# An FFN unit reads its first kept half before the rounding of its last weight block, every other one into a second buffer

## What is computed

```python
def swiglu(h, w_up, w_down):
    gate, up = jnp.split(h @ w_up, 2, axis=-1)
    return (jax.nn.silu(gate) * up) @ w_down
```

## Time and profile before

| | us |
|---|---|
| median of three runs | 941.75 |
| lowest, highest | 941.49, 942.89 |
| the profiled execution, its own time | 946.19 |
| its span, first to last instruction | 944.4 |
| PE busy | 921.6 (98%) |
| DVE busy | 669.7 (71%) |
| ACT busy | 446.7 (47%) |
| POOL busy | 107.8 (11%) |

### The profile page before, as it was taken

The page is one execution under the profiler, slowest core; times in us unless marked ns, Lnnn a source line. Parts: engine busy times, 40 slices in busy tenths (PEclk is TensorE's granted clock), DMA queues, the critical chain, the costliest instruction groups (busy, mean ns, idle before and its releaser), DMA issues.

```text
span 944.4 us, 22445 instructions
## 1 busy us (share of the span) xinstructions
PE 921.6 (98%) x9425; PEld 894.1 (95%) x9425; DVE 669.7 (71%) x1254; ACT 446.7 (47%) x824; POOL 107.8 (11%) x135
## 2 busy tenths in 40 slices
PE   5999999999999999999999999999999999999997
PEld 5899888999999999999999999999999999999997
DVE  3678878875567767477766888999435899994454
ACT  6588345423334554663222257565322666653223
POOL 0101011211120110100100001222001222220000
PEclk9999999999999999999999999999999999999998
DMA  9825233434343432315743232332333343323312
GB/s 348 267 67 156 59 88 84 143 104 136 103 129 102 125 87 69 101 47 145 238 124 111 85 96 68 87 93 73 86 97 105 98 119 97 91 78 94 91 51 95
DMA packets 146031, 104.82 MB, mean 111 GB/s; under 512 B 5153, under 2 KB 138855, under 8 KB 144779
## 3 DMA queue, kind: packets, MB, share of 16 engines
q1 hardware_dynamic: 138955, 79.16, 28.7%
q0 software_dynamic: 6352, 22.00, 7.5%
q10 hardware_dynamic: 624, 2.23, 0.6%
HBM read 100.06 MB, written 3.31 MB: 109 GB/s over the span
## 4 chain that ended last, share of the span: by engine, by line
PE 90%; DVE 4%; ACT 3%; issue 2%; DMA 0%; ACTq 0%; DVEq 0%
PE G L2216 58%; PE G L2311 19%; PE R L2224 12%; PE R L2227 1%; DVE cy L1887 1%; DVE cy L1884 1%; DMA xtok<-in_x_prompt 0%; DVE cy L1888 0%; DVE cy L1883 0%; ACT w_hi L1258 0%; DVE w_sum L1752 0%; DVE sum_lo L1761 0%; ACT L1274 0%; DVE relT L1934 0%; ACT inp L1274 0%
## 5 line engine op out<-in xcount | busy, mean ns | idle before, releaser
L2216 PE MATMUL G<-h_hi,w_hi 128*128 128x272 f32 (+1 forms) x880 | 264.4, 300 | 0.2 <-DVE ff_shift L2162 0.2
L2216 PE MATMUL G<-h_lo,w_hi 128*128 128x272 f32 (+1 forms) x880 | 254.5, 289 | 0.4 <-issue 0.4
L2216 PE MATMUL G<-h_hi,w_lo 128*128 128x272 f32 (+1 forms) x880 | 254.2, 289 | 0.0
L1645 DVE TENSOR_TENSOR w_lo<-raw,w_hi 128x1024 fp32r<-128x1024 f32 (+3 forms) x111 | 118.6, 1069 | 82.1 <-ACT w_hi L1258 81.4
L2216 PEld LDWEIGHTS G<-h_hi,w_hi 128*128 128x128 f32 x880 | 166.5, 189 | 3.2 <-DVE ff_shift L2162 0.4
L2216 PEld LDWEIGHTS G<-h_lo,w_hi 128*128 128x128 f32 x880 | 166.7, 189 | 0.6 <-issue 0.6
L2216 PEld LDWEIGHTS G<-h_hi,w_lo 128*128 128x128 f32 x880 | 166.4, 189 | 0.0
L1258 ACT ACTIVATE w_hi<-raw 128x1024 fp32r<-128x1024 f32 (+3 forms) x111 | 101.5, 914 | 114.1 <-PE G L2216 113.9
L2311 PE MATMUL G<-x_hi,sum_hi 128*128 128x272 f32 x288 | 83.8, 291 | 1.6 <-ACT partial L1369 1.5
L2311 PE MATMUL G<-x_hi,sum_lo 128*128 128x272 f32 x288 | 83.4, 290 | 0.0
L2311 PE MATMUL G<-x_lo,sum_hi 128*128 128x272 f32 x288 | 83.0, 288 | 0.0
(11 more groups left out here) (335 smaller groups left out, 2117.2 us busy)
## 6 DMA issues: line engine op xcount, KB each, us to landing
raw<-in_w_in SPq DMA_DIRECT2D x48, 512.0 KB, 4.1
raw<-in_w_up SPq DMA_DIRECT2D x44, 512.0 KB, 4.0
w_ada<-in_w_ada_t POOLq DMA_DIRECT2D x49, 256.0 KB, 3.2
wada<-in_w_ada_s SPq DMA_DIRECT2D x8, 1024.0 KB, 14.3
raw<-in_w_down SPq DMA_DIRECT2D x14, 384.0 KB, 3.4
raw<-in_w_down SPq DMA_DIRECT2D x16, 320.0 KB, 3.2
raw<-in_w_out SPq DMA_DIRECT2D x8, 512.0 KB, 4.0
w_ada_t<-in_w_ada_t POOLq DMA_DIRECT2D x15, 256.0 KB, 3.2
```

The source lines that it names most:

```text
L1645: dve.tensor_tensor(lo, raw[:, i % RAW, 0:job.nk, 0:job.m], hi.bitcast(F32), ALU.subtract).then_inc(w_lo_done, 1)
L2216: ins = pe.matmul(out, w, x, start=(job.first and k == 0 and p == 0), stop=(job.last and k == job.nk - 1 and p == 2))
```

## The change

Reading 0 moves ahead of the rounding of `d` and of `q_ahi` in all units (it stood there in unit 1). Odd units keep it in `acc[:, 0:272]` instead of `partial[:, 0, :]`, so reading 0 of unit u waits for `q_c11` of unit u-2 instead of unit u-1. In unit 0, reading 3 goes ahead of the rounding of sum 2 of unit 1 (and of its sum and of the low part of sum 1, which are on VectorE).

```diff
             for p in range(len(PRODUCTS)):
                 do("q_mul", u, p)
-            if u == 1:
-                do("q_read", u, 0)
+            do("q_read", u, 0)
             if u > us[0]:
                 do("q_a", u - 1, 0)
                 do("q_hi", u, "d")
                 do("q_ahi", u - 1)
                 do("q_lo", u, "d")
                 do("q_alo", u - 1)
-            if u != 1:
-                do("q_read", u, 0)
             if soon:
                 do("q_read", u, 1)
...
             if not soon:
                 do("q_read", u, 2)
+            if u == 0:
+                do("q_read", u, 3)
             if nxt is not None:
                 do("q_add", nxt, 2)
                 do("q_lo", nxt, 1)
                 do("q_hi", nxt, 2)
             do("q_c12", u)
-            if soon:
+            if u == 1:
                 do("q_read", u, 3)
...
+        def kept(u, r):
+
+            return acc[:, 0:HALF] if r == 0 and u % 2 else partial[:, r, :]
...
                     act.wait_ge(q_done, 7 * u + READS[r] + 1)
-                    if u:
-                        act.wait_ge(q_out, 3 * (u - 1) + (3, 2, 1, 2)[r])
-                    else:
+                    before = u - (2 if r == 0 else 1)
+                    if before >= 0:
+                        act.wait_ge(q_out, 3 * before + (3, 2, 1, 2)[r])
+                    elif u == 0:
                         wait_slot(act, groups_before[0] - 1)
-                    act.activation(partial[:, r, :], q_bank(u, "y" if r == 1 else "x"), ACT.Copy).then_inc(q_kept, 1)
+                    act.activation(kept(u, r), q_bank(u, "y" if r == 1 else "x"), ACT.Copy).then_inc(q_kept, 1)
```

More of the change, by code:

```diff
@@ L1766, in _ @@
                     dve.wait_ge(q_kept, 4 * u + 3)
-                    dve.tensor_tensor(q_halves(g_act[:, u % 2, :])[1], q_bank(u, "y"), partial[:, 2, :], ALU.add)\
+                    dve.tensor_tensor(q_halves(g_act[:, u % 2, :])[1], q_bank(u, "y"), kept(u, 2), ALU.add)\
                         .then_inc(q_out, 1)
@@ L1771, in _ @@
                     dve.wait_ge(q_kept, 4 * u + 4)
-                    dve.tensor_tensor(q_halves(val[:, a_no(u) % 2, :])[1], partial[:, 3, :], partial[:, 1, :], ALU.add)\
+                    dve.tensor_tensor(q_halves(val[:, a_no(u) % 2, :])[1], kept(u, 3), kept(u, 1), ALU.add)\
                         .then_inc(q_out, 1)
@@ L1776, in _ @@
                     dve.wait_ge(q_done, 7 * u + 6)
-                    dve.tensor_tensor(q_halves(g_act[:, u % 2, :])[0], q_bank(u, "z"), partial[:, 0, :], ALU.add)\
+                    dve.tensor_tensor(q_halves(g_act[:, u % 2, :])[0], q_bank(u, "z"), kept(u, 0), ALU.add)\
                         .then_inc(q_out, 1)
```

## The result

The changed kernel takes 949.94 us median of 6 runs (948.82 to 950.83) against 942.32 us for the kernel before in the same comparison (941.24 to 946.19, 6 runs): a ratio of 1.0074, 95% interval 1.0062 to 1.0085. That is 7.0 us of 942.3, within 5.8 to 8.0.

What follows compares the result with a forecast made beforehand. PE's matmul stream (98% busy) was taken as the bound, with a chain over other engines just longer in steady units. 5.0 + 0.9 + 0.6 = +6.5 us on 941.75 gave 948.2 us, range 945.3 to 950.0.

Steps and rivals of the forecast that it cites:

- The sum: Whole kernel: 5.0 + 0.9 + 0.6 = +6.5 us, giving 948.2 us on the median of 941.75.
- The second buffer, 0: Reading 0 no longer waits for the previous unit's q_c11, but the silu ahead on ACT covers that wait: 0 us.
- Reading 0 ahead of d, +0.50 in ten units: Units 7 to 16: d_hi 0.68 us later, w_lo and product 6 0.50 later; +5.0 us, bounds 4.3 and 6.8.
- the two ways in which DVE and POOL could meet: At POOL's sum 1, steady units: DVE's activation low part first, w_lo 0.50 us later; or POOL first, 0.43 later.
- Units 2 to 4, +0.9: 0.77 us won ahead of unit 2's product 2, but the d chain is delayed as in steady units: +0.9 us.
- the bounds -0.9 and +1.5: Units 2 to 4: three units at -0.3 us each, or at +0.50 us each.
- Reading 3 of unit 0, +0.6: Unit 0's 0.37 us wait at product 6 goes, none kept; unit 1 loses more: +0.6 us, bounds -0.4 and +0.7.
- the predicted pair of gaps: Unit 1: product 2 still waits until about 618.8; product 3 waits till 620.95 and restarts, +0.66 us.
- The first (faster): Gaps at the readings count, later d costs nothing, unit 1's gap goes: about 2.4 us faster, 939.3 us; chance 0.07.
- The second: Steady units lose nothing, DVE and POOL not excluding each other; only unit 2's gap is won: 941.0 us; chance 0.11.
- The third's gap: Gaps at products 3 and 4 add to product 6's, ten times 0.25 us more: 950.7 us; chance 0.08.
- A sign of being wrong, badly put: Units 7 to 16: wrong if product 6's distance stays 10.7 us or POOL's start is independent of DVE's preceding instruction.

Runs made afterwards that it cites:

- e1: The second buffer alone, every step in its old place, against the kernel before: 942.65 us, ratio 0.9994.
- e9: Kernel before plus second buffer; reading 3 before sum 4's rounding, reading 0 between roundings (units 2-5), unit 1's reading 0 before silu, reading 1 before d: ratio 0.9972.
- e2: Reading 0 ahead of the rounding of d in all units, one buffer, reading 3 of unit 0 unmoved, against the kernel before: 948.71 us, ratio 1.0058.
- e4: The changed kernel with d's rounding ahead of reading 0 again, reading 0 still ahead of the activation's rounding: 943.65 us, ratio 1.0008 to the kernel before.
- e8: The changed kernel with the activation's low part moved behind DVE's sum 4 where a unit has a successor: 943.76 us, ratio 1.0013 to the kernel before.
- e3: Only unit 0's reading 3 moved ahead of the rounding, against the kernel before: 943.27 us, ratio 0.9996.
- e10: The changed kernel with reading 1 too ahead of d's rounding in units 2 to 5 and 7 to 17: 970.98 us, ratio 1.0298 to the kernel before.
- e5: The kernel before with reading 3 ahead of the rounding of sum 4: 941.77 us, ratio 0.9993.

## Why the prediction was right

- **The sum.** +6.5 us was predicted from rows of the kernel before; 6.43 us stands in the stages and 7.0 us (5.8 to 8.0) in the comparison. 949.94 lies 1.7 above the predicted 948.2, and 0.6 of that is the median of before, 942.32 here for 941.75. The other 1.1 us does not stand in the stages; the executions of one kernel spread by 2 to 5 us.
- **The second buffer, 0.** Shown by e1: -0.03 us. That the silu covers its wait agrees with e9, where reading 0 stands ahead of the silu and the gap goes; the same move without the buffer was not run.
- **Reading 0 ahead of d, +0.50 in ten units.** 0.49 us from POOL's start to w_lo's end, 0.49 us from unit to unit; 4.97 us in the stage for 5.0. The reading began 0.33 us behind product 0's last matmul (0.32 predicted), POOL's sum spanned 1.79, and of the two ways in which DVE and POOL could meet it was the one that was taken: DVE's low part came in 0.08 us ahead. e2 shows the order as the cause, e4 that d's rounding is the step in question, and e8 that POOL's span follows the order of DVE's instructions.
- **Units 2 to 4, +0.9.** e2 has it alone: 67.30 - 66.44 = 0.86. But +0.9 was a choice between the bounds -0.9 and +1.5, so that it fits to 0.04 is in part luck. By distances of product 6, unit 2 of the changed kernel pays 0.15 us, unit 3 0.56 and unit 4 0.19. In unit 2 the gap of 0.77 ahead of product 2 went, but one of 0.41 came ahead of product 3. In unit 4 a gap of 0.28 ahead of product 2 (651.86 behind 651.45), which the prediction had not seen, went too.
- **Reading 3 of unit 0, +0.6.** e3: +0.56, with the predicted pair of gaps.
- **The rivals.** The first (faster) fell with POOL's span. The second asked for DVE and POOL not to exclude each other; e8 and the 1.57 us low part in unit 1 speak against it. The third's gap exists: product 4 of unit 7 starts at 746.67 behind 746.49, 0.18 for 0.125, because of reading 2, but it lies within the later one at product 6, as the forecast had it, and costs nothing more. It is why product 6 starts only 0.49 behind the matmul before it where a gap of about 0.7 was expected: of the 0.64 us by which the unit is longer than PE's own 10.57, 0.44 stand at product 6 and the rest at products 3 and 4.
- **What was not priced.** The prediction took the meeting of POOL's sum 3 and DVE's sum 4 as unchanged. The order was unchanged, but its margin fell from 0.49 to 0.20 us; e10 shows that 0.95 us a unit hung on it. The price of this change was small because that order held.
- **A sign of being wrong, badly put.** The prediction would be wrong "if POOL's start does not depend on the DVE instruction before it". POOL's start does not: it comes 0.46 us behind product 1's last matmul (743.88 for 743.42), as it did before (0.47). It is POOL's end that depends on DVE, and this is what the sum used.

## What to carry to other kernels

An in-order engine that is half idle can still hold the critical chain: ask of every instruction moved ahead of others whether it has to wait, and who waits for the ones behind it. Here ACT waited 0.34 us and then read, so that d_hi came 0.72 us later behind the silu; that cost 0.49 us a unit on PE, by way of two other engines, although in these units the reading had not been late. A buffer pays only if nothing else in the queue waits for the same event. And where two engines exclude each other, note which one arrives first and by how much. Measured here against POOL's sum 1, a low part that ended 0.16 us later (e4) cost nothing and one that ended 0.67 us later (the change) cost 0.49; a delay that reversed the order at sum 3 and sum 4 (e10) cost 0.95 at that one place.

## What was not expected of the hardware

- A product that waits costs PE twice: the wait, and about 0.06 to 0.11 us behind the first matmul (0.18 to 0.24 us to the second one instead of 0.125), in every gap read here, even where the wait itself is below 0.02 us, as at product 2 in e5.
- DVE and POOL: in all twelve traces a sum on POOL that had to wait ended 1.14 to 1.17 us behind DVE's end, one that had not spans 1.26 to 1.31. A DVE subtraction or sum of 128x512 that had to wait for POOL ended 0.53 to 0.56 us behind POOL's end, a w_lo 1.07 to 1.10. So a hold that overlaps POOL's start by no more than 0.13 us is free (e4: DVE's end 0.13 behind POOL's start, a span of 1.30). The Trainium skill, "SBUF — State Buffer", section "SBUF: two separate sides", has the first come take the shared port for its whole instruction, and the trace agrees with whole instructions blocked (1.57 and 1.63 us for 0.68).
- The steady units repeat closely, 10.70 to 10.72 us in the kernel before and 11.19 to 11.25 in the changed one, so that a change of 0.1 us a unit is seen in one trace where six runs of the whole kernel spread by 2 us (changed) and 5 us (before).
